# Mean and inverse deviation of five norms as full 128 x 512 tiles: products of 512 columns with a block of ones, and ScalarE's Ln and Exp, in place of 64-column pieces and rows

## The reference

```python
def layer_norm(x, g, b):
    mu = jnp.mean(xf, axis=-1, keepdims=True)
    var = jnp.mean(jnp.square(xf - mu), axis=-1, keepdims=True)
    return ((xf - mu) * lax.rsqrt(var + LN_EPS) * g + b)
def hybrid_layer(x, ...):                      # twice
    mix = (three mixers of x @ w_in) @ w_o
    x = layer_norm(DEEPNORM_ALPHA * x + mix, ln1_g, ln1_b)
    u_act, u_gate = jnp.split(x @ ffn_w_up, 2, axis=-1)
    hid = jax.nn.gelu(conv(u_act)) * u_gate
    x = layer_norm(DEEPNORM_ALPHA * x + hid @ ffn_w_down, ln2_g, ln2_b)
def rms_norm_2(x, g):
    y = xf * lax.rsqrt(jnp.mean(xf * xf, axis=-1, keepdims=True) + EPS)
# second_block, twice: x += gate * mixer(modulate(rms_norm_2(x))); x += gate * mlp(modulate(rms_norm_2(x)))
# and a last rms_norm_2
```

## Time and profile before

| | us |
|---|---|
| median of 3 runs (2383.82 to 2385.04) | 2384.8 |
| the profiled execution | 2385.51 |
| its span, first to last instruction | 2383.7 |
| PE busy | 2316.6 (97%) |
| DVE busy | 1376.8 (58%) |
| ACT busy | 995.1 (42%) |
| POOL busy | 242.9 (10%) |

### The profile page before, as it was taken

One profiled execution on the slowest core, in us unless ns is written; L12 is line 12 of the kernel. 1 busy time (PEld: TensorE's weight loads), 2 busy tenths in 40 slices (PEclk: granted clock), 3 DMA queues, 4 the chain that ended last, 5 costly groups with the idle time before them and its releaser, 6 DMA issues.

```text
span 2383.7 us, 35801 instructions
## 1 busy us (share of the span) xinstructions
PE 2316.6 (97%) x13448; PEld 1865.0 (78%) x13448; DVE 1376.8 (58%) x1904; ACT 995.1 (42%) x1543; POOL 242.9 (10%) x192
## 2 busy tenths in 40 slices
PE   8999999999999999999999999999999999999998
PEld 6777767888887777767888877777888888888887
DVE  4678676666445578676666447565344356543443
ACT  5667244333245657244233334754233243322332
POOL 0042220000031032220000030201000010000002
PEclk9999999999999999999999998999999999999999
DMA  4210015656432210015556331222222221232222
GB/s 162 80 62 28 29 63 174 194 189 194 132 106 71 88 62 29 29 63 177 192 194 194 125 112 46 81 89 98 95 97 94 95 96 63 89 97 97 97 97 88
DMA packets 68796, 248.33 MB, mean 104 GB/s; under 512 B 7632, under 2 KB 8144, under 8 KB 68688
## 3 DMA queue, kind: packets, MB, share of 16 engines
q1 hardware_dynamic: 68688, 246.85, 31.5%
HBM read 244.72 MB, written 2.10 MB: 104 GB/s over the span
## 4 chain that ended last, share of the span: by engine, by line
PE 88%; DVE 5%; ACT 4%; issue 2%; POOL 0%; DMA 0%; DVEq 0%; ACTq 0%; SPq 0%
PE dense L602 25%; PE dense L604 24%; PE dense L603 24%; PE aux L710 2%; ACT wh L1406 1%; PE aux L893 1%; PE aux L911 1%; PE aux L1014 1%; PE aux L602 1%; PE aux L1025 1%; DVE wl L2069 1%; PE aux L881 1%; PE aux L1110 1%; PE aux L603 1%; PE aux L604 1%
## 5 line engine op out<-in xcount | busy, mean ns | idle before, releaser
L602 PE MATMUL dense<-xh,wh 128*128 128x512 f32 x1840 | 736.8, 400 | 24.2 <-DVE wl L2069 10.5
L1406 ACT ACTIVATE wh<-raw 128x1024 fp32r<-128x1024 f32 x346 | 366.7, 1060 | 932.3 <-PE dense L604 925.2
L603 PE MATMUL dense<-xl,wh 128*128 128x512 f32 x1840 | 718.4, 390 | 0.0
L604 PE MATMUL dense<-xh,wl 128*128 128x512 f32 x1840 | 718.4, 390 | 0.0
L2069 DVE TENSOR_TENSOR wl<-raw,wh 128x1024 fp32r<-128x1024 f32 x346 | 426.4, 1232 | 459.0 <-ACT wh L1406 457.4
L602 PEld LDWEIGHTS dense<-xh,wh 128*128 128x128 f32 x1840 | 346.6, 188 | 123.5 <-issue 29.2
L603 PEld LDWEIGHTS dense<-xl,wh 128*128 128x128 f32 x1840 | 346.7, 188 | 73.9 <-issue 5.7
L604 PEld LDWEIGHTS dense<-xh,wl 128*128 128x128 f32 x1840 | 346.5, 188 | 73.0
L602 PE MATMUL dense<-hidh,wh 128*128 128x512 f32 x928 | 363.6, 392 | 4.9 <-DVE hidl L2101 2.1
L604 PE MATMUL dense<-hidh,wl 128*128 128x512 f32 x928 | 361.8, 390 | 0.0
L603 PE MATMUL dense<-hidl,wh 128*128 128x512 f32 x928 | 361.7, 390 | 0.0
(11 more groups left out here) (400 smaller groups left out, 2411.8 us busy)
## 6 DMA issues: line engine op xcount, KB each, us to landing
raw<-stream SPq DMA_DIRECT2D x362, 512.0 KB, 3.4
mraw<-mod_stream SPq DMA_DIRECT2D x96, 512.0 KB, 4.2
x<-x_t SPq DMA_DIRECT2D x4, 512.0 KB, 7.0
y_t<-x SPq DMA_DIRECT2D x8, 256.0 KB, 2.0
cst<-consts SPq DMA_DIRECT2D x1, 993.0 KB, 9.3
band<-bands SPq DMA_DIRECT2D x1, 576.0 KB, 4.3
cond<-c_rows SPq DMA_DIRECT2D x1, 512.0 KB, 10.5
pv_next<-vecs SPq DMA_DIRECT2D x3, 82.5 KB, 4.3
```

What stands on the lines that cost most here:

```text
L602: pe.matmul(o, a, h, start=first, stop=False)
L603: pe.matmul(o, a, l, start=False, stop=False)
L604: return pe.matmul(o, b, h, start=False, stop=last)
L1406: act.activation(wh[:, slot].rearrange("p k m -> p (k m)"), raw[:, slot, :], ACT.Copy).then_inc(hi_done, 1)
```

## The change

Five norms, 0 to 3 and 5 (`WIDE`), get their statistics as whole 128 x 512 tiles. Norms 4, 6, 7 and 8 stay as they were. GpSimd now adds all 8 tiles (`SUMS`, `SQ_SUMS`), and in norms 0 and 2 DVE adds 8 squares. GpSimd waits for the residual addition of the tile instead of for ACT's square of it. TensorE does two float32 products of a 128 x 128 block of ones with `norm_sum` and with `norm_sq`, 512 columns each. ACT copies the mean to SBUF (`mean_t`) and squares it (`var_t`). DVE centres with `mean_t`, makes the variance in place over 512 columns, ACT takes Ln and then Exp with scale -0.5 into `rstd_t`. The tile phase reads `mean_t` and `rstd_t` from SBUF where it read two PSUM banks. Norm 5 issues the product of `norm_sum` too, whose result it doesn't use. The diff also brings functions for a deferred form of a norm. `DEFERRED` is empty, and none of them issues an instruction.

```diff
+DEFERRED = ()
+WIDE = (0, 1, 2, 3, 5)
+SUMS = (8, 8, 8, 8, 7, 8, 7, 0, 7)
+SQ_SUMS = (7, 8, 7, 8)
...
+            def spread(k, square):
+
+                if k in (0, 2) and square:
+                    pe.wait_ge(sq_added, sq_sums_before(k) + 7)
+                elif k < 4 and square:
+                    pe.wait_ge(sq_added, sq_sums_before(k) + 8)
+                else:
+                    pe.wait_ge(sums_tile, sums_before(k) + 8)
+                pe.matmul(aux[4 if square else 5][:], const("ones"),
+                          norm_sq[:] if square else norm_sum[:], start=True, stop=True)\
+                    .then_inc(sums_pe if square else mean_pe, 1)
...
+                if k in WIDE:
+                    spread(k, False)
+                    spread(k, True)
...
+            def mean_stats(k):
+
+                act.wait_ge(mean_pe, k + 1)
+                act.activation(mean_t[:], aux[5][:], ACT.Copy, scale=1.0 / D)\
+                    .then_inc(mean_ready, 1)
+                act.activation(var_t[:], aux[5][:], ACT.Square, scale=1.0 / D)\
+                    .then_inc(mean_ready, 1)
+
+            def root_stats(k):
+
+                act.wait_ge(var_ready, k + 1)
+                act.activation(var_t[:], var_t[:], ACT.Ln).then_inc(sd_ready, 1)
+                act.wait_ge(sd_ready, k + 1)
+                act.activation(rstd_t[:], var_t[:], ACT.Exp, scale=-0.5).then_inc(rstd_ready, 1)
...
+                if k != 0 and k != 2:
+                    act.preload_act_table_set(LN_EXP)
+                mean_stats(k)
+                root_stats(k)
...
+            def variance_tile(k):
+
+                if k < 4:
+                    dve.wait_ge(mean_ready, 2 * k + 2)
+                    dve.wait_ge(sums_pe, k + 1)
+                    chain(stt(var_t[:], aux[4][:], 1.0 / D, var_t[:], MUL, SUB))
+                    ts(var_t[:], var_t[:], 0.0, LN_EPS, ALU.max, ADD).then_inc(var_ready, 1)
+                else:
+                    dve.wait_ge(sums_pe, k + 1)
+                    ts(var_t[:], aux[4][:], 1.0 / D, RMS_EPS, MUL, ADD).then_inc(var_ready, 1)
...
-                    dve.wait_ge(mean_pe, k + 1)
-                tt(x[:, m, :], x[:, m, :], aux[5][:], SUB).then_inc(centred_x, 1)
+                    dve.wait_ge(mean_ready, 2 * k + 1)
+                tt(x[:, m, :], x[:, m, :], mean_t[:], SUB).then_inc(centred_x, 1)
...
+                stt(nt[:, m % 2, :], x[:, m, :], gain, rstd_t[:] if wide else aux[4][:], MUL, MUL)\
+                    .then_inc(n_mul, 1)
```

More of the change, by code:

```diff
@@ L697, in section, with deferred @@
+            def deferred(pl, s, n, k, count, tile):
+                ahead_pair(pl, s, n, k)
+                turned_pair(pl, s + 2, n, tile)
+                with pe.Fori(3, count // 2) as i:
+                    for j in range(2):
+                        dense(pl, s + j, i, xh, xl)
             def section(pl, s, count, h, l, tiles=KT, tile_sem=None, tile_at=0):
@@ new lines, in ahead_lo, with ahead_out @@
+            def ahead_lo(k, m, gain):
+                h, l = (xh, xl) if k in IN_PLACE else (hidh, hidl)
+                dve.wait_ge(xh_ready, highs_before(k) + m + 1)
+                stt(l[:, m, :], x[:, m, :], gain, h[:, m, :].bitcast(F32), MUL, SUB)\
+                    .then_inc(xl_ready, 1)
+            def ahead_out(k, pl, s, j, also=None):
+                dve.wait_ge(pe_chunk, pl.chunk(s + j) + 1)
+                v = small[:, 12, 4 * j:4 * j + 4]
+                if k < 4:
+                    for n in range(2):
+                        t = column(v, n, 8 * j + n, 8 * j + 2 + n)
+                    chain(t)
+                    if also is not None:
+                        tt(v[:, 2:3], v[:, 1:2], also, MUL)
+                    chain(stt(ahead_t[:, j, :], mean_t[:], v[:, 0:1], AHEAD[j][:], MUL, ADD))
+                    tt(ahead_t[:, j, :], ahead_t[:, j, :], rstd_t[:], MUL).then_inc(ahead_ready, 1)
+                else:
+                    column(v, 1, 8 * j, 8 * j + 1)
+                    tt(ahead_t[:, j, :], AHEAD[j][:], rstd_t[:], MUL).then_inc(ahead_ready, 1)
@@ L2227, in projections @@
                     low(cl[r, t, :], src, ch[r, t, :], cl_ready)
-                for s in range(C_SB + 2, C_WAG):
+                for s in range(C_SB + 2 + behind, C_WAG):
                     refill(pl, s)
@@ L2770, in up @@
                             hidl_ready)
-                    if first:
-                        early(q)
+                    if first and deferral:
+                        for i in range(2):
+                            for j in range(2):
+                                up(i, j)
+                    elif first:
+                        for j in range(2):
+                            early_half(q, j)
                         for j in range(2):
```

721 lines of the change are left out of this document (510 added, 211 removed).

## The result

| | before | after |
|---|---|---|
| median | 2384.31 us (4 runs, 2381.72 to 2385.04) | 2405.33 us (4 runs, 2403.77 to 2406.82) |
| ratio | 1 | 1.009, 95% interval 1.0078 to 1.0103 |
| span of the profiled execution | 2383.7 us | 2405.0 us |

The kernel became 21.0 us (0.9%) slower. The prediction said 15.6. The direction and the range were right, and the size was short by 5.4.

The account below looks back on a forecast made before the run. TensorE holds 88% of the chain, so a norm costs time only where TensorE lacks dense work. Norm 0 2.2, norm 1 3.5, norm 2 3.85, norms 3 and 4 1.8, norm 5 4.2: 2384.8 + 15.6 = 2400.4 us, range 2392 to 2407.

Parts of the forecast that it names:

- Part 1, the way to T: Last addition of x to first scaling: norms 0, 1, 2, 3, 5 change by -0.3, +1.3, +1.35, +1.3, +3.0 us.
- T minus E: First scaling's start minus end of last x addition; predicted near 8.5 in norms 0 and 2, 8.1 in 1 and 3.
- the turns: GpSimd and two-SBUF-input DVE instructions alternate instead of running together; a turn costs DVE about 1.1 us.
- Part 2, the tile phase: Norms 0, 1, 2: DVE's two SBUF inputs contend with GpSimd's low parts; +2.5, +2.2, +2.5 us.
- third low part: GpSimd's low part of tile 5 in norms 0 to 2, predicted to end 13.5 us after the first scaling, not 11.1.
- the same, +1.3: Norm 3's way to the first scaling was said to repeat norm 1's, +1.3 us.
- costs nothing: ACT's table load in norms 1 and 3, behind the last square while TensorE's product is awaited: 0 us.
- A table load that comes in at norms 4 and 6 stands ahead of a wait: New table loads at norms 4 and 6 were said to precede a wait; no cost was added.
- Part 3, the clock: TensorE idles more, so half clock: norms 1 and 2 0, norm 4's sums +0.5, norm 5 +1.2 us (0 to 3).
- my 3.0 for the rest: Norm 5's way to first scaling: eighth sum of squares and the unused product ahead, +3.0 us.
- longer low clock: Rival: low stretches in norms 1, 2 and 5 outlast TensorE's slack, 2 us each; 2406.4 us, 17%.

Follow-up runs that it names:

- e2: Kernel after plus 22 unread 64 x 64 x 64 products in each of norms 0 and 1; 2404.9 us, ratio to before 1.0079.
- e9: Kernel after plus 11 unread 64 x 64 x 64 products in each of norms 0 and 1; 2407.9 us (1 run).
- e10: Kernel after with the sums of norms 0 to 3 in two products each (7 tiles, then the last), no eighth additions; 2398.5 us (1 run).
- e1: Kernel after with mean and inverse deviation written to and read from PSUM banks; 2402.4 us, ratio to before 1.0066.
- e3: Kernel after with norm 3's table load ahead of shift_h and norm 4's square root load behind the last square; 2404.8 us (1 run).
- e5: Kernel after plus four unread 512-column products ahead of norm 5's two products of sums; 2406.9 us (1 run).
- e8: e7 with VectorE centring one tile, not three, ahead of the variance; 2378.9 us, ratio to before 0.9970.
- e6: Kernel after with two-step sums (norms 0-3), PSUM statistics, e3's table loads, 20 + 20 unread short products, norm 5 as before; 2384.9 us, ratio to before 1.0000.
- e7: e6 with norm 4's eight squares also through the block of ones, 512 columns each; 2383.4 us, ratio to before 0.9998.

## Why the prediction was right, and where it was short

**Part 1, the way to T, norms 0, 1 and 2: the numbers right, in part by luck.** Predicted -0.3, +1.3, +1.35; measured -0.55 (9.32 to 8.77), +1.21 (7.08 to 8.29), +1.29 (7.15 to 8.44). I had both products of norms 1 and 2 at full clock. At full clock T minus E is 7.9 in both (e2 and e9), so the five 512-column instructions and the turns cost only 0.75 each, and the other 0.5 was the half clock that I had put at nothing there. In norm 2 GpSimd's eighth addition ended at E + 1.73 and not at the E + 2.19 that I laid out. In norm 1 I took E for 717.47, from the square behind it; it was 717.17, so the wait before was 7.08 and not 6.8. e10 shows what counts: without the eighth addition, and with the full clock that goes with it, 8.8, 8.3 and 8.4 become 7.1 to 7.2.

**Part 2, the tile phase: right, a little high.** Predicted +2.5, +2.2, +2.5, from a third low part at T + 13.5; measured T + 13.26, +2.16 each. e1 shows the turns as its cause. The rule of the Trainium skill's page "SBUF — State Buffer", section "Who interferes with whom", by which GpSimd would block VectorE for its whole length (3.3 per norm as I worked it out), overstates it here: the scaling at 351.82 loses 1.0 us, not 1.3, and the norm 2.16.

**Norm 3 in part 1: the step that failed.** I wrote "the same, +1.3" and that the table load "costs nothing". It was +3.03, 1.7 more. Norm 3 is norm 1 but for one thing: ScalarE has `shift_h` ahead of its table load, and `shift_h` waits for VectorE's small addition `mod`. (Norm 1 has a `mod` held just as long, and nothing waits for it.) I looked at what is large. The addition of 0.2 us reads SBUF twice, was held for GpSimd's sum of squares to 1.26, and pushed `shift_h`, load and mean. e10 gives the addition alone (0.20), e3 the load alone (1.43).

**"A table load that comes in at norms 4 and 6 stands ahead of a wait": wrong at norm 4, right at norm 6.** Norm 4's root has two waits ahead of it in the code, and in the trace the load was released by the variance: 1.28 in the trace, 1.27 back in e3. At norm 6 the root has one wait, and the load runs at 2011.33, ahead of the variance at 2012.44; the shift at norm 6's root is +21.55, as in front of it. That the number of waits makes the difference is inferred from these two cases.

The Trainium skill's page "ScalarE: Activation LUTs", section "What ACT_TABLE_LOAD costs", adds a drain of about 1.38 us to such a load. No run here shows one: the root starts at 1468.38, 0.01 behind the end of the load, and e3 gave back the length of the load and no more.

**Part 3, the clock: right in kind, too small.** Norm 4's sums began at half clock, as predicted, and stayed there for nearly all of the 64 pieces (13.8 us instead of 13.05): of the 5.05, 3.03 went to T and 1.28 to the load, so 0.74 is left for the sums and rows (+0.5 predicted). In norms 1 and 2 I put it at 0: in the tile phases that held, on the way to T it was 0.5 each. In norm 5 I took 1.2 out of 0 to 3; in the profile after it was 2.8 (by e5), near my upper bound: 1.8 in the two products (3.8 us instead of 2.0) and 1.0 in the tile phase. With my 3.0 for the rest that gives 5.8, the measured value. The other five executions give 0.7 to 1.8 and all six 1.5 in the mean, so 1.2 was a fair value, and this one execution drew a long one.

**What I had not thought of: the mixers of layer 2, +3.02.** The change takes 22 short products out of each of norms 0 and 1, and so moves what lies behind in TensorE's stream. I counted their time and not their place.

**The sum.** The misses are +1.7 (`mod` and the load behind it), +1.3 (table), +0.2 (norm 4's sums), +1.6 (norm 5), +3.0 (mixers), against -0.6, 0 and -0.15 in norms 0 to 2 and -1.3 ahead of norm 0: +5.8 on 15.6. With 0.1 ahead of norm 5 that is the shift of 21.5 behind it. That -1.3 hid part of the error. The rival "longer low clock" gave 2406.4, but mostly not for its reason: the low stretches in norms 1 and 2 cost 0.5 each ahead of T, already inside the numbers of part 1, and nothing to speak of in the tile phases, where the rival had them. That the range held is luck in part: its upper part was built of other costs of like size.

What stays open: why 22 to 44 products fewer make the stops. The place is not all of it, since in layer 1's mixers, where all these kernels have the same code and the same place, there are one to four stops of 0.2 to 1.2 us, other ones from kernel to kernel; in layer 2's the two groups never overlapped in 13 profiles.

## What to carry to other kernels

A broadcast sum by a block of ones is a good form, if the last tile goes into PSUM straight from its producer and no side engine has to add it first; the idea was 21 us slower with the eighth addition and statistics in SBUF, and 7 us faster in e8, without either, with norm 5 in its old form, norm 4 in the new one, and table loads, centrings and short products placed anew. Statistics that VectorE reads beside a busy GpSimd belong in PSUM, and a small instruction with two SBUF inputs is a long one if something waits for it. Before calling a table load hidden, see which wait it carries; and before calling unchanged code unaffected, look for "issue" stops inside runs of very short products.

## What the runs showed of the hardware

- TensorE stopped for 0.19 to 1.19 us inside runs of float32 products of 64 partitions by 64 or 128 columns (30 passes of 64 columns in 0.66 us), waiting for nothing that the profile shows; in layer 2 this went with how many instructions lay ahead. The Trainium skill's page "Runtime: NRT & Kernel Launch", section "Instruction fetch mechanics", calls instruction fetch hidden by the pace of issue. These stops speak against it for such short products, if fetch is what they are.
- The granted clock fell in an idle time of 4.19 us (0.50 in 1646 to 1650) and did not with 3.60 us of unread products in it. With 0.8 us idle and four products of 512 columns (e6, e7, e8) it never fell ahead of T. With 2.51 us idle the first product behind took anything from 1.13 us (full clock) to 2.08 (half) in the same code.
- An addition of 48 columns with two inputs in SBUF took 0.20 us alone and 1.26 beside GpSimd.
